# A two-block transformer kernel: a reordered, chunk-fed start, and the rotary exchange of halves moved from matmuls to on-chip DMA

## The reference

```
xn = rms(x) * norm_attn;  proj = xn @ w_in            # one wide projection, split 14 ways
o_a = forgetting attention, 8 heads of 128 (q, k normed, decay from log_sigmoid(f_logit + bias))
o_b = sparse attention, 8 heads of 192 (compressed + selected + window branch, 3 gates each)
x = x + (sigmoid(gate_a) * (o_a @ w_up_fox) + sigmoid(gate_b) * (o_b @ w_up_nsa)) @ w_out
x = x + (silu(hn @ w_gate) * (hn @ w_up)) @ w_down
```

```
def _rotate(x, ang):                       # on each 64 of the 128 channels
    x1, x2 = jnp.split(x, 2, axis=-1)      # halves of 32 channels
    return concat([x1 * cos - x2 * sin, x2 * cos + x1 * sin])
```

## Time and profile before

| | us |
|---|---|
| median of 3 runs | 2602.21 |
| the profiled execution | 2598.55 |
| its span | 2596.7 |

### The profile page before, as it was taken

One profiled execution on the slowest core, in us unless ns is written; L12 is line 12 of the kernel. 1 busy time (PEld: TensorE's weight loads), 2 busy tenths in 40 slices (PEclk: granted clock), 3 DMA queues, 4 the chain that ended last, 5 costly groups with the idle time before them and its releaser, 6 DMA issues.

```text
span 2596.7 us, 51591 instructions
## 1 busy us (share of the span) xinstructions
PE 2524.1 (97%) x20012; PEld 2461.2 (95%) x20012; DVE 1451.2 (56%) x2211; ACT 1170.0 (45%) x1663; POOL 132.7 (5%) x176
## 2 busy tenths in 40 slices
PE   6999999999999999999999999999999989999996
PEld 4999999999999999999999999999998979999996
DVE  4666434675565555455554556555554456765645
ACT  4555323543454444333443445544444345555532
POOL 2000210000001000000000001000000100000002
PEclk9999989999999999999999999999999999999998
DMA  6556755446666666666666657544443635645552
GB/s 182 161 159 163 189 150 137 115 130 168 173 183 189 181 186 184 193 180 180 191 187 180 184 166 213 160 133 135 133 139 97 167 98 155 170 131 137 143 153 70
DMA packets 806850, 411.92 MB, mean 159 GB/s; under 512 B 48132, under 2 KB 802624, under 8 KB 806464
## 3 DMA queue, kind: packets, MB, share of 16 engines
q1 hardware_dynamic: 803216, 397.47, 55.6%
q0 software_dynamic: 2944, 10.49, 1.3%
q10 hardware_dynamic: 576, 2.36, 0.2%
HBM read 408.17 MB, written 2.10 MB: 158 GB/s over the span
## 4 chain that ended last, share of the span: by engine, by line
PE 89%; DVE 4%; issue 3%; ACT 3%; DMA 0%; SPq 0%; DVEq 0%; ACTq 0%; POOL 0%; POOLq 0%
PE ps_unit L245 26%; PE ps_unit L247 26%; PE ps_unit L246 26%; DVE w_lo L232 1%; PE ps_score L554 1%; ACT w_hi L225 1%; PE ps_score L971 1%; PE ps_out L815 0%; PE ps_norm L815 0%; DVE work L348 0%; DVE work L2370 0%; PE ps_score L794 0%; PE ps_turn L794 0%; PE ps_score L775 0%; PE ps_score L599 0%
## 5 line engine op out<-in xcount | busy, mean ns | idle before, releaser
L232 DVE TENSOR_TENSOR w_lo<-raw,w_hi 128x1024 fp32r<-128x1024 f32 (+2 forms) x764 | 891.9, 1209 | 254.4 <-ACT w_hi L225 254.3
L225 ACT ACTIVATE w_hi<-raw 128x1024 fp32r<-128x1024 f32 (+2 forms) x764 | 769.1, 1038 | 438.6 <-PE ps_unit L247 437.8
L245 PE MATMUL ps_unit<-b_hi,w_hi 128*128 128x256 f32 (+1 forms) x3184 | 910.7, 286 | 5.9 <-DVE w_lo L232 5.9
L247 PE MATMUL ps_unit<-b_hi,w_lo 128*128 128x256 f32 (+1 forms) x3184 | 905.8, 284 | 0.0
L246 PE MATMUL ps_unit<-b_lo,w_hi 128*128 128x256 f32 (+1 forms) x3184 | 904.2, 284 | 0.0
L245 PE MATMUL ps_unit<-a_hi,w_hi 128*128 128x256 f32 (+2 forms) x2816 | 811.6, 288 | 7.9 <-DVE w_lo L232 7.5
L246 PE MATMUL ps_unit<-a_lo,w_hi 128*128 128x256 f32 (+2 forms) x2816 | 803.3, 285 | 0.0
L247 PE MATMUL ps_unit<-a_hi,w_lo 128*128 128x256 f32 (+2 forms) x2816 | 802.8, 285 | 0.0
L245 PEld LDWEIGHTS ps_unit<-b_hi,w_hi 128*128 128x128 f32 x3184 | 601.6, 189 | 11.8 <-issue 5.1
L247 PEld LDWEIGHTS ps_unit<-b_hi,w_lo 128*128 128x128 f32 x3184 | 602.2, 189 | 0.0
L246 PEld LDWEIGHTS ps_unit<-b_lo,w_hi 128*128 128x128 f32 x3184 | 599.5, 188 | 0.7
(11 more groups left out here) (386 smaller groups left out, 1708.4 us busy)
## 6 DMA issues: line engine op xcount, KB each, us to landing
raw<-in_w_in SPq DMA_DIRECT2D x152, 512.0 KB, 4.8
raw<-in_attn_w_in SPq DMA_DIRECT2D x96, 512.0 KB, 4.6
raw<-in_gla_w_in SPq DMA_DIRECT2D x96, 512.0 KB, 4.7
raw<-in_w_ffn_gate SPq DMA_DIRECT2D x88, 512.0 KB, 4.7
raw<-in_w_ffn_up SPq DMA_DIRECT2D x88, 512.0 KB, 4.5
raw<-in_w_ffn_down SPq DMA_DIRECT2D x64, 512.0 KB, 4.7
raw<-in_w_out SPq DMA_DIRECT2D x32, 512.0 KB, 4.7
raw<-in_attn_w_out SPq DMA_DIRECT2D x32, 512.0 KB, 4.7
```

What stands on the lines that cost most here:

```text
L225: act.activation(hi[:, b % 4, 0:size], raw[:, b % 8, 0:size], ACT.Copy)\
L232: dve.tensor_tensor(lo[:, b % 4, 0:size], raw[:, b % 8, 0:size], hi[:, b % 4, 0:size], ALU.subtract).then_inc(lo_ready, 1)
L245: pe.matmul(dst, wh, xh[:, k0 + k, 0:N], start=start and k == 0, stop=False)
L247: mm = pe.matmul(dst, wl, xh[:, k0 + k, 0:N], start=False, stop=stop and k == kb - 1)
```

## The change

Two changes are made together.

**Start.** The loads are reordered: the identity columns of the constants, the attention gain alone, the weights of the first two units, the k unit of head 0, and then the rest. `x` comes in four pieces of 512 columns, each with its own semaphore. `U_B0` and `U_B0+1` become one unit of 40 columns (24 gates, 8 logits), laid as a strip of stride 40, of which TensorE reads 128 columns at a time; it and the q unit of head 0 are multiplied chunk by chunk, as soon as a chunk's low part is there. The other gains and the meta tokens are transposed at chunk 10. The table of logarithm and exponential is loaded first.

**Rotation.** `ga_perm` is gone; SyncE exchanges the groups of 32 partitions of `axn` by four DMAs from SBUF to SBUF, and VectorE multiplies by the sine in one instruction on SBUF.

```diff
-U_FOX = U_B0 + 2
+U_FOX = U_B0 + 1
...
+        def ga_swap(sp, j):
+            sp.wait_ge(aq_n, j + 1)
+            if j:
+                sp.wait_ge(aq_r, j)
+            for q in range(4):
+                src, dst = slice(32 * (q ^ 1), 32 * (q ^ 1) + 32), slice(32 * q, 32 * q + 32)
+                sp.dma_start(arot[dst], axn[src, :, 0:T]).then_inc(aq_perm, 16)
...
-            for n, b in enumerate((psT[0], psT[1], psN)):
-                mm = pe.matmul(b[:, 0:T], swap, axn[:, n, 0:T], start=True, stop=True)
-            mm.then_inc(aq_perm, 1)
...
-            dve.wait_ge(aq_perm, j + 1)
-            for n, b in enumerate((psT[0], psT[1], psN)):
-                dve.tensor_tensor(arot[:, n], b[:, 0:T], sin, ALU.mult)
+            dve.wait_ge(aq_perm, 64 * j + 64)
+            dve.tensor_tensor(arot, arot, sin.unsqueeze(1).broadcast_to([P, 3, T]), ALU.mult)
...
                         load_unit(sp, ga_unit(j, 2 + m), 0, 0, w_ai, c)
+                        if j and m == 3:
+                            ga_swap(sp, j - 1)
...
+            sp.dma_start(con[:, 0:P], const[:, 0:P]).then_inc(s_con, 16)
+            sp.dma_start(va_in[0:16, :], ...norm_attn...).then_inc(s_con, 16)
+            for h in range(2):
+                k = slice(h * HB, (h + 1) * HB)
+                low = raw[:, 2 * h, 0:HB * LOW].rearrange("p (k m) -> p k m", m=LOW)
+                sp.dma_start(low[:, :, 0:32], w_in[:, k, C_NG:C_NG + 32]).then_inc(raw_full[2 * h], 16)
+                sp.dma_start(low[:, :, 32:LOW], w_in[:, k, C_F:C_F + 8]).then_inc(s_low, 16)
+                load_block(sp, U_FOX - 1 + h, 1, 0, 0, w_in[:, k, C_FQ:C_FQ + P], first=True)
+            load_unit(sp, U_FOX + 1, 0, 0, w_in, C_FK, first=True)
+            sp.dma_start(con[:, P:N_K], const[:, P:N_K]).then_inc(s_va, 16)
... (the other gains, the small loads, then v and gate of head 0)
+            turn_x(0)
+            turn_x(1)
+            for kc in range(KC):
+                if kc + 2 < KC:
+                    turn_x(kc + 2)
+                if kc == 10:
+                    ... (waits for all gains; 2 transposes of gains, 16 of the meta tokens)
+                pe.wait_ge(c_lo, kc + 1)
+                h, k = divmod(kc, HB)
+                for s, w in ((0, LOW), (1, P)):
+                    ... (3 matmuls into psU[s]; the block's low part awaited at k == 0)
             pe_norm(pe, 0, T)
-            mm_unit(pe, U_B0 + 1, 0, 0, AH, AL, w=24)
...
+            ln_exp_table(act)
...
                 act_square(act, kc, kc % 2, kc, T, wait=kc >= 2)
+                if kc in (1, 5):
+                    b = 0 if kc == 1 else 2
+                    act.wait_ge(s_low, 48)
+                    hi_block(act, b, HB * LOW + P - LOW)
+                    hi_block(act, b + 1)
+                if kc in (10, 13):
+                    hi_block(act, 4 + (kc == 13))
...
                     dve_chunk(dve, kc - 1, kc - 1, V_ATTN, AH, AL, T)
+                if kc in (2, 6):
+                    ... (lo_block of the same two blocks)
+                if kc in (11, 14):
+                    lo_block(dve, 4 + (kc == 14))
+                if kc == 13:
+                    vectors()
```

More of the change, by code:

```diff
@@ L360, in act_norm, with hi_block, lo_block @@
             invert_rms(act, [(RS[:, 0:N], psN[:, 0:N])], s_rs, k)
-        s_con, s_va, s_vb, s_x = sem("con_in"), sem("va_in"), sem("vb_in"), sem("x_in")
+        s_con, s_va, s_vb = sem("con_in"), sem("va_in"), sem("vb_in")
+        s_x, s_low = [sem(f"x_in{n}") for n in range(4)], sem("low_in")
+        LOW = 40
+        def hi_block(act, b, size=HB * P):
+            act.wait_ge(raw_full[b % 8], 16 * (b // 8 + 1))
+            if b >= 4:
+                act.wait_ge(block_done, b - 3)
+            act.activation(hi[:, b % 4, 0:size], raw[:, b % 8, 0:size], ACT.Copy).then_inc(hi_ready, 1)
+        def lo_block(dve, b, size=HB * P):
+            dve.wait_ge(hi_ready, b + 1)
+            dve.tensor_tensor(lo[:, b % 4, 0:size], raw[:, b % 8, 0:size], hi[:, b % 4, 0:size],
+                              ALU.subtract).then_inc(lo_ready, 1)
         s_vbz, s_vt, s_v = sem("vb_zero"), sem("vec_turned"), sem("vec_ready")
@@ L1752, in _, with turn_x @@
         def _(pe):
-            pe.wait_ge(s_con, 16)
-            pe.wait_ge(s_va, 16 * 14)
-            pe.wait_ge(s_vb, 16 * 7)
-            pe.transpose(psT[0][:, 0:N_VA], va_in[0:N_VA, :], ident[0:N_VA, 0:N_VA])
-            pe.transpose(psT[0][:, P:P + N_VB], vb_in[0:N_VB, :], ident[0:N_VB, 0:N_VB]).then_inc(s_vt, 1)
-            pe.wait_ge(s_x, 32)
-            for kc in range(KC):
+            pe.wait_ge(s_con, 32)
+            pe.transpose(psT[0][:, 0:16], va_in[0:16, :], ident[0:16, 0:16]).then_inc(s_vt, 1)
+            def turn_x(kc):
+                pe.wait_ge(s_x[kc // 4], 16 if kc < 12 else 32)
                 if kc >= 4:
@@ L1781, in fox @@
                     fox_turn(pe, h - 1)
+                else:
+                    pe.wait_ge(evacuated, U_B0 + 1)
+                    for t in range(2):
+                        mm = pe.transpose(psT[1][:, 32 * t:32 * t + 24], ngr[:, t * P:(t + 1) * P],
+                                          ident[0:24, 0:24])
+                    mm.then_inc(ng_t, 1)
                 mm_unit(pe, *u[2], AH, AL)
@@ L1794, in fox @@
                 mm.then_inc(fx_vt, 1)
-            pe.wait_ge(evacuated, U_B0 + 2)
-            for t in range(2):
-                mm = pe.transpose(psT[1][:, 32 * t:32 * t + 24], fz[:, 2, t * P:(t + 1) * P],
-                                  ident[0:24, 0:24])
-            mm.then_inc(ng_t, 1)
-            pe.wait_ge(ng_c, 1)
             fox(0)
@@ L2188, in fox @@
                 cf.begin(h, 1, -1)
-                split_lo(dve, u[1], 4, h)
+                if not first:
+                    split_lo(dve, u[1], 4, h)
                 done(dve, u[0], 4, h)
@@ L2200, in fox @@
                 evac(dve, u[1], 4, h, kr)
+                if first:
+                    dve.wait_ge(fx_za, 3)
+                    st.link(dve.tensor_scalar(zm, z, 0.0, None, ALU.min))
+                    st.link(dve.tensor_tensor(zm, zm, zl, ALU.subtract))
+                    st.link(dve.tensor_tensor_scan(c_row, ones[0:FOX_H, :], zm, 0.0, ALU.mult, ALU.add))
+                    dve.wait_ge(ng_t, 1)
+                    dve.tensor_copy(gtok[:, :, :],
+                                    psT[1][:, 0:64].rearrange("p (t n) -> p t n", t=2)[:, :, 0:24])\
+                       .then_inc(ng_c, 1)
                 split_lo(dve, u[3], 4, h)
@@ L2434, in _ @@
         def _(pool):
+            for b in (0, 2):
+                ins = pool.memset(raw[:, b, HB * LOW:HB * LOW + P - LOW], 0.0)
+            ins.then_inc(s_low, 16)
             pool.memset(fcm, 0.0)
```

145 lines of the change are left out of this document (82 added, 63 removed).

## The result

The changed kernel took 2578.56 us, the median of 4 runs (2575.3 to 2582.67), against 2601.4 us for the kernel before on the same chip (2600.07 to 2602.66): ratio 0.9913, 95% interval 0.9896 to 0.993. The profiled execution has a span of 2575.5 us, 21.2 less than before.

What follows compares the result with a forecast made beforehand. TensorE, busy 2524.1 of 2596.7 us, was taken as the bound. Start 18.1 plus rotation 9.1 gave 27.2 us, so 2602.21 - 27.2 = 2575.0 us; main case 2569 to 2580, eight in ten 2567 to 2589.

Steps and rivals of the forecast that it cites:

- Bound and mark: Start: the TensorE-bound stream behind the k unit, which begins at 59.2 us, moves forward by as much as that unit.
- The rotation: Second block's attention: dropping the permutation matmuls saves 1.30 us in each of seven rounds, 9.1 us; ends 0 and 10.4.
- the rotation ends just before them already; there I count nothing: Last attention round: scores come after 24 matmuls, not 48, with the rotation ending just before; no gain counted.
- the prediction's own sign: Rotation: VectorE's sine product idle above 0.5 us, ended by a DMA, would prove the prediction wrong.
- the rival in which the exchange comes too late: Rotation: exchange landing at 5 us or more wins nothing, 2584 us, 8%; worse, at 9 us, 2616 us, 3%.
- The start: From first loads to k unit: it begins at 41.1 in place of 59.2, 18.1 us less; bounds 11 and 21.
- First full chunk: Start: first weights there at 13.5 us, then splits; TensorE has its first full chunk at 16.3.
- I take 0.85 for one: Start's loads: 0.85 us for each narrow load, 3.4 for four, within the sum putting first weights at 13.5.
- Loop: Start's loop over chunks: from the first full chunk at 16.3 to the loop's end at 38.4 us.
- it is through at 34.5 and does not set the end: Chunk loop: VectorE's 18.2 us of work ends at 34.5; its inserted pieces hold TensorE up 1 us in all.
- the late weights: Start: first weights at 17 instead of 13.5, VectorE's pieces exposed; start worth 11, total 20, 2582 us; chance 15%.
- The slow clock: Chunk loop: TensorE stays at 1.2 GHz until the loop's end, 11 us lost, 2586 us; chance 12%.

Runs made afterwards that it cites:

- e2: Kernel before with only the rotation's exchange by four SBUF-to-SBUF DMAs added, the start as before; 2594.57 us, ratio 0.9979.
- after_again: The changed kernel run once more, unedited, in a later set of 4 runs; 2578.31 us, ratio 0.9931.
- e4: Changed kernel with the exchange of heads 0 to 6 issued behind the next unit's two 512 KB loads; 2592.75 us, ratio 0.997.
- e5: Changed kernel without the four narrow loads, their place filled with zeros on GpSimd; 2575.46 us, ratio 0.9904.
- e10: e9 with the third and fourth pieces of x issued by SyncE behind the q blocks; 2571.54 us, ratio 0.9898.
- e7: Changed kernel with TensorE's transposes of x three chunks ahead of the products instead of two; 2573.98 us, ratio 0.9898.
- e8: Changed kernel with GpSimd's squares and adds covering one column instead of 256 after the first chunk; 2579.09 us, ratio 0.9908.
- e1: Changed kernel with the permutation by matmuls and the rotation from PSUM put back, so the start alone; 2586.19 us, ratio 0.9944.
- e9: Changed kernel with the second half's narrow load waited for apart and transposes of x three chunks ahead; 2573.28 us, ratio 0.9904.
- e6: Changed kernel with head 0's q blocks in ScalarE's queue behind x's first two pieces, second half's narrow load waited for apart; 2577.68 us, ratio 0.9912.

## Why the prediction was right, and where it was off

**Bound and mark.** That TensorE's stream moves as a whole with the k unit held, but for 0.4 us: the gates' two transposes, which stood ahead of the q unit, now lie between the k and the v unit, and the v unit is evicted 6.1 us after the k unit in all traces with the new start, where it was 5.7.

**The rotation: 9.1 us predicted, 9.1 measured in seven rounds, 8.3 at the last scores.** Each of the seven gained 1.30 us in the changed kernel and 1.29 in e2 alone. The four issues took 2.67 us and not 1.6, but the landing took 2.2 and not 2.8, and there was slack for both. The Trainium skill, "DMA: Bandwidth & Descriptors", Anatomy of one DMA, gives its fixed part of about 2 us for DMAs that GpSimd issues; the 2.2 us of L799, issued by SyncE, agree with it. What failed is "the rotation ends just before them already; there I count nothing", of the last round. The exchange came too late there: with norm, four issues (2.5 us), landing and three instructions of 0.95 to 0.96 one behind the other, the sine product waited 1.7 us for a DMA and TensorE 1.9 us for VectorE, and 0.8 us were lost (0.7 in `after_again`, 1.6 in e2). By the prediction's own sign, idle time above 0.5 us that a DMA ends, it was wrong in this round and right in the seven others. So the rival in which the exchange comes too late is a true mechanism; e4 made it happen in every round, and it cost 1.7 us a round at a landing of 4.0 us.

**The start: 18.1 us predicted, 15.2 measured without a slow stretch in the loop, 13.4 with one.** The missing 2.9 us are three terms, read from `after_again`, less the 0.1 us by which the norm was quicker:

- *First full chunk, 16.3 predicted, 17.81 measured: 1.5 us.* The failed step is "I take 0.85 for one" and the division of bytes by 386 GB/s, which gave weights at 13.5. They were complete at 15.0 (15.2 in the first profile). While the small rows were moved, the engines were full at 166 GB/s; without the narrow loads, in e5, they moved 238 in the same window. The rule of the Trainium skill quoted beside the sum ("DMA: Bandwidth & Descriptors", Specifications) was borne out by these two figures; the sum should have used a rate of such rows. e5 and e10 show what the landing of the q block hangs on: without the narrow loads it comes 1.0 us earlier, without the second megabyte of x ahead of it 3.3.
- *Loop, 22.1 predicted, 23.35 measured (17.81 to the norm's matmul at 41.16): 1.2 us.* The failed step is "it is through at 34.5 and does not set the end", with 1 us for all that VectorE holds up. VectorE's last low part began at 39.7. Its work was counted rightly, 17.8 us busy in the loop against 18.2 in the sum. Not counted was its idle time, 5.5 us, of which transposes by TensorE ended 4.2. The two engines run in each other's wait: VectorE waits for TensorE's transposes, which stand behind products that wait for VectorE, 3.9 us in all. One more step of lead took 2.9 us off the k unit's start (e7), and GpSimd's adds, beside which low parts grew from 0.48 to up to 0.97 us, were worth 1.4 (e8). That only 1.2 us are missing is in part luck: TensorE's own work, 23.35 less the waits of 3.9, took 19.4 us where the sum had 21.1. Chunk 10's 18 transposes took 1.5 us and not 2.2, and a chunk with its transposes 0.94 (27.86 to 28.80 in the changed kernel) and not 1.15. Two errors, of 2.9 and of 1.7 us, worked against each other.
- *The k unit itself, 5.68 predicted, 5.95 measured: 0.3 us,* since it starts after a hole. The 2.7 us of norm and hand-overs were 2.6, with no table load among them.

So of the rivals the late weights came nearest in kind, at about half their size. The slow clock did not stay: TensorE had its fast level 5.5 us after the first full chunk, and 4.7 in `after_again`, against 4.9 in the prediction. It came back, late in the loop in the changed kernel's profile, where it cost 1.6 us, and in the k unit in five others, at 1.5 us each: six of eleven profiles with the new start have a small form of that rival. Nor were the v and gate weights issued "at about 13 us": SyncE came to them at 24.05, and TensorE did not wait for them.

**The sum.** The two parts give 15.2 + 9.1 = 24.3 us at these marks, or 22.5 with the slow stretch, against 22.8 and 19.7 measured in time. What else the spans hold lies behind the k unit's eviction and behind the last norm sum. Put side by side eviction by eviction, all thirteen traces run alike, within 0.1 us but for the 0.4 above, until 230 us behind the k unit's eviction, and within 0.2 again from 370 us on to the first norm sum. Between the two lies the compression with its neighbours, where nothing was changed. Their windows in the profiles of before, e2 and `after_again` (the value before the last two is the granted clock):

```profile
290.00:450.00 160.00, 159.07 (x1161) 153.78 (x1160) 58.86 (x65) 41.49 (x53) 20.47 (x29) 0.87 0.59 152
```

```profile
290.00:450.00 160.00, 160.00 (x1136) 155.18 (x1135) 55.25 (x61) 41.32 (x53) 20.50 (x29) 0.84 0.59 151
```

```profile
290.00:450.00 160.00, 159.21 (x1126) 153.45 (x1126) 61.91 (x93) 43.47 (x64) 13.27 (x22) 0.86 0.56 142
```

The clock falls there for short stretches, more of them in one execution than in another. From the k eviction to the first norm sum before took 1573.8 us, e2 1577.7, e1 1579.8, the changed kernel 1572.6 and 1576.7, and the others 1573.5 to 1579.9; from the last norm sum to the end it is 635.0 us before and 632.0 to 637.9 in the others. Two profiles of one kernel differ by 4.1 us, so such a difference can be chance in single profiles; before lies inside the spread of the others. Start, this way, rounds and end close the account of both profiles: 15.2 - 2.9 + 9.0 - 0.3 = 21.0 us of the span in `after_again`, 13.4 + 1.2 + 9.1 - 2.5 = 21.2 in the first. For e2 no riddle is left, since 7.4 us lie inside the interval of its timed gain. Whether a shift of the work by some us makes these stretches more frequent stays open, as no run repeats one kernel's profile often enough.

## What to carry to other kernels

Price loads at the front by the rate at which their rows move while the other loads run, not by the best rate of the trace, and ask of each early load what it takes from the ones that the first product waits for: half of x, moved behind the first weights, brought the k unit forward by 3.3 us (e10 against e9). In a loop where two engines feed each other, count each one's waits for the other and not only its busy time; one more step of lead recovered 2.9 us at the k unit's start here, and kept a head start that otherwise was lost. Look at the last round of a pipeline by itself: with less work to hide behind, the exchange that had slack in seven rounds was waited for in the eighth. Judge an effect of a few us by the distance of two marks in the trace, as single executions of one kernel differed by 4 us in parts that no edit touched.

## What was unexpected of the hardware

- SyncE stood for 4.3 to 4.7 us at the issue at 2.77 us, whether it was a 512 KB block or a narrow load, for 3.9 us with half of x moved away, and for 5.4 us behind two blocks without narrow loads (e5).
- 32 KB in rows of 32 B, issued at 2.14 us, took 10.1 us to land beside x, and 14.9 with the two q blocks between the pieces of x (e6).
- Four exchanges of 96 KB from SBUF to SBUF took 0.60 to 0.67 us each to issue, and landed 2.2 us later on a quiet queue, 4.0 (median) behind weight blocks.
- VectorE's two-input instruction of 0.48 us took up to 0.97 beside GpSimd's adds, and 0.49 at most without them (e8).
- TensorE's lower clock came back for some 3 us around the k unit in six of eleven profiles, at 1.5 to 1.6 us each, behind a loop in which it had waited again and again for VectorE.
